# Streamed weights: low part written over the loaded words, five loaded and four rounded places, each unit split one unit earlier

## The reference

```python
# first block, each of 2 layers (z, the context, is carried too in the first)
x = x + 0.5 * mx[2] * swiglu(modulate(rms_norm(x), mx[0], mx[1]), ffn1_w1[l], ffn1_w3[l], ffn1_w2[l])
hx = modulate(rms_norm(x), mx[3], mx[4]) @ w_in[l]
...                                   # neighbourhood, gated linear, grouped-query attention, Fourier mixing
x = x + mx[5] * (mix_x @ w_out[l])
x = x + 0.5 * mx[8] * swiglu(modulate(rms_norm(x), mx[6], mx[7]), ffn2_w1[l], ffn2_w3[l], ffn2_w2[l])
# second block, each of 2 layers
h = h + jnp.einsum('blc,cd->bld', mix, w_out)          # forgetting attention and retention
h = h + swiglu of rmsnorm(h)
```

## Time and profile before

| what | value |
|---|---|
| median of 3 runs | 2449.03 (2448.18 to 2449.29) |
| span of the profiled execution | 2444.0 |
| PE busy | 2386.3 (98%) |
| DVE busy | 1510.9 (62%) |
| ACT busy | 1002.4 (41%) |
| POOL busy | 394.3 (16%) |
| share of PE in the chain that ended last | 90% |
| mean granted TensorE clock | 0.998 |

### The profile page before, as it was taken

The page is one execution under the profiler, slowest core; times in us unless marked ns, Lnnn a source line. Parts: engine busy times, 40 slices in busy tenths (PEclk is TensorE's granted clock), DMA queues, the critical chain, the costliest instruction groups (busy, mean ns, idle before and its releaser), DMA issues.

```text
span 2444.0 us, 39330 instructions
## 1 busy us (share of the span) xinstructions
PE 2386.3 (98%) x15054; PEld 2096.5 (86%) x15054; DVE 1510.9 (62%) x2546; ACT 1002.4 (41%) x1645; POOL 394.3 (16%) x403
## 2 busy tenths in 40 slices
PE   7999999999999999999999999999999999999998
PEld 4888888777888888888888878999888999989998
DVE  5878765784699855523323585665666665666664
ACT  4222334644522223422222465545445444446443
POOL 2221211240122221111011130121000220000220
PEclk9999999999999999999999999999999999999999
DMA  8566542112366664233322222555433555434554
GB/s 330 196 210 212 177 150 87 61 61 82 105 222 230 241 219 155 87 96 102 96 95 95 87 78 77 185 181 183 151 110 128 173 173 179 148 114 139 190 189 138
DMA packets 97879, 362.49 MB, mean 148 GB/s; under 512 B 11024, under 2 KB 11280, under 8 KB 96560
## 3 DMA queue, kind: packets, MB, share of 16 engines
q1 hardware_dynamic: 75744, 274.42, 34.0%
q0 software_dynamic: 21968, 85.72, 10.2%
HBM read 359.04 MB, written 1.05 MB: 147 GB/s over the span
## 4 chain that ended last, share of the span: by engine, by line
PE 90%; DVE 3%; ACT 3%; issue 2%; DMA 1%; POOL 0%; ACTq 0%; DVEq 0%; POOLq 0%
PE bank L746 28%; PE bank L748 27%; PE bank L747 27%; ACT ring_high L1241 1%; PE bank L1026 1%; DVE ring_low L1713 1%; PE bank L996 1%; PE bank L1014 1%; PE bank L1048 1%; PE bank L967 0%; PE bank L975 0%; DMA arena<-w_mod_first_dram 0%; PE bank L1191 0%; PE bank L1104 0%; DVE arena L1779 0%
## 5 line engine op out<-in xcount | busy, mean ns | idle before, releaser
L1713 DVE TENSOR_TENSOR ring_low<-ring,ring_high 128x1024 fp32r<-128x1024 f32 x524 | 649.9, 1240 | 553.1 <-ACT ring_high L1241 551.1
L746 PE MATMUL bank<-x_parts,ring_high 128*128 128x512 f32 (+2 forms) x2700 | 912.4, 338 | 14.2 <-DVE ring_low L1713 10.5
L748 PE MATMUL bank<-x_parts,ring_low 128*128 128x512 f32 (+2 forms) x2700 | 899.8, 333 | 0.0
L747 PE MATMUL bank<-x_parts,ring_high 128*128 128x512 f32 (+2 forms) x2700 | 898.6, 333 | 0.0
L1241 ACT ACTIVATE ring_high<-ring 128x1024 fp32r<-128x1024 f32 x524 | 551.6, 1054 | 628.9 <-PE bank L748 628.4
L746 PEld LDWEIGHTS bank<-x_parts,ring_high 128*128 128x128 f32 x2700 | 510.1, 189 | 80.3 <-issue 18.1
L748 PEld LDWEIGHTS bank<-x_parts,ring_low 128*128 128x128 f32 x2700 | 510.2, 189 | 48.1
L747 PEld LDWEIGHTS bank<-x_parts,ring_high 128*128 128x128 f32 x2700 | 510.1, 189 | 47.0 <-issue 0.2
L609 POOL TENSOR_TENSOR hidden_parts<-fresh,hidden_parts 128x512 fp32r<-128x512 f32 (+2 forms) x132 | 215.0, 1628 | 1354.5 <-ACT hidden_parts L1360 1354.5
L746 PE MATMUL bank<-hidden_parts,ring_high 128*128 128x512 f32 (+2 forms) x1122 | 368.1, 328 | 0.3 <-POOL hidden_parts L609 0.3
L748 PE MATMUL bank<-hidden_parts,ring_low 128*128 128x512 f32 (+2 forms) x1122 | 367.3, 327 | 0.0
(11 more groups left out here) (232 smaller groups left out, 2130.0 us busy)
## 6 DMA issues: line engine op xcount, KB each, us to landing
ring<-stream_dram SPq DMA_DIRECT2D x521, 512.0 KB, 3.4
mod_ring<-w_mod_dram POOLq DMA_DIRECT2D x128, 512.0 KB, 4.8
arena<-w_mod_first_dram POOLq DMA_DIRECT2D x8, 1024.0 KB, 10.3
ring<-stream_dram POOLq DMA_DIRECT2D x3, 512.0 KB, 10.7
arena<-na_bias_dram POOLq DMA_DIRECT2D x2, 768.0 KB, 11.4
mod_ring<-consts_dram POOLq DMA_DIRECT2D x1, 1140.0 KB, 5.4
resid<-x_dram POOLq DMA_DIRECT2D x2, 512.0 KB, 6.0
resid<-ctx_dram POOLq DMA_DIRECT2D x2, 512.0 KB, 7.2
```

The source lines that it names most:

```text
L746: pe.matmul(out, w[0][:, b], xh, start=start, stop=False)
L747: pe.matmul(out, w[0][:, b], xl, start=False, stop=False)
L748: return pe.matmul(out, w[1][:, b], xh, start=False, stop=stop)
L1713: dve.tensor_tensor(low[:, u % RING], ring[:, u % RING], high_f[:, u % RING], ALU.subtract).then_inc(low_parts, 1)
```

## The change

It keeps five places for loaded words and four for the rounded high part. The low part is written over the loaded words, so the ring takes nine places in SBUF as before. ACT and DVE split up to four units ahead. SP loads unit u when PE has used unit u - 5. SP's loop over the stream becomes straight-line code. At the start, two units instead of one are split before the first ffn1 goes on.

```diff
-RING = 3
+LOADED = 5
+SPLIT = 4
+FIRST_UNITS = 3
...
-        ring = sb("ring", RING * UNIT).rearrange("p (s n) -> p s n", s=RING)
-        high = sb("ring_high", RING * UNIT, F32R)
-        low = sb("ring_low", RING * UNIT, F32R)
+        ring = sb("ring", LOADED * UNIT).rearrange("p (s n) -> p s n", s=LOADED)
+        low = sb("ring_low", LOADED * UNIT, F32R, over=place_of["ring"]).rearrange("p (s n) -> p s n", s=LOADED)
+        high = sb("ring_high", SPLIT * UNIT, F32R)
...
-            turns = UNITS // RING
-            with sp.Fori(1, turns) as turn:
-                for s in range(RING):
-                    sp.wait_ge(low_parts, turn * RING + (s + 1 - RING))
-                    sp.dma_start(ring[:, s], A["stream"][turn * RING + s]).then_inc(unit_loaded[s], 16)
...
+            for u in range(FIRST_UNITS, UNITS):
+                if u >= LOADED:
+                    sp.wait_ge(*when("unit_used", u - LOADED))
+                sp.dma_start(ring[:, u % LOADED], A["stream"][u]).then_inc(unit_loaded[u % LOADED], 16)
...
-                while split[0] < min(split[1] + RING, UNITS):
+                while split[0] < min(split[1] + SPLIT, UNITS):
                     u = split[0]
                     split[0] += 1
-                    if u >= RING:
-                        act.wait_ge(*when("unit_used", u - RING))
+                    if u >= SPLIT:
+                        act.wait_ge(*when("unit_used", u - SPLIT))
...
-                    dve.tensor_tensor(low[:, u % RING], ring[:, u % RING], high_f[:, u % RING],
+                    dve.tensor_tensor(low[:, u % LOADED], ring[:, u % LOADED], high_f[:, u % SPLIT],
                                       ALU.subtract).then_inc(low_parts, 1)
...
-                    split_ahead(1)
+                    split_ahead(2)
```

More of the change, by code:

```diff
@@ L262, in build @@
         eps_one = sb("eps_one", 2)
-        ring = sb("ring", RING * UNIT).rearrange("p (s n) -> p s n", s=RING)
-        high = sb("ring_high", RING * UNIT, F32R)
-        low = sb("ring_low", RING * UNIT, F32R)
-        high_f = high.bitcast(F32).rearrange("p (s n) -> p s n", s=RING)
-        high = high.rearrange("p (s n) -> p s n", s=RING)
-        low = low.rearrange("p (s n) -> p s n", s=RING)
+        ring = sb("ring", LOADED * UNIT).rearrange("p (s n) -> p s n", s=LOADED)
+        low = sb("ring_low", LOADED * UNIT, F32R, over=place_of["ring"]).rearrange("p (s n) -> p s n", s=LOADED)
+        high = sb("ring_high", SPLIT * UNIT, F32R)
+        high_f = high.bitcast(F32).rearrange("p (s n) -> p s n", s=SPLIT)
+        high = high.rearrange("p (s n) -> p s n", s=SPLIT)
         xr = sb("x_parts", 2 * KC * N1, F32R)
@@ L353, in scalar2 @@
             return small[0:rows, at:at + 1]
-        unit_loaded = [sem(f"unit_loaded{i}") for i in range(RING)]
+        unit_loaded = [sem(f"unit_loaded{i}") for i in range(LOADED)]
         high_parts = sem("high_parts")
@@ L560, in _ @@
             sp.wait_ge(*when(f"first_mod_loaded{(KC - 1) % FIRST_SLOTS}", KC - 1))
-            turns = UNITS // RING
-            with sp.Fori(1, turns) as turn:
-                for s in range(RING):
-                    sp.wait_ge(low_parts, turn * RING + (s + 1 - RING))
-                    sp.dma_start(ring[:, s], A["stream"][turn * RING + s]).then_inc(unit_loaded[s], 16)
-            for u in range(turns * RING, UNITS):
-                sp.wait_ge(low_parts, u - RING + 1)
-                sp.dma_start(ring[:, u % RING], A["stream"][u]).then_inc(unit_loaded[u % RING], 16)
+            for u in range(FIRST_UNITS, UNITS):
+                if u >= LOADED:
+                    sp.wait_ge(*when("unit_used", u - LOADED))
+                sp.dma_start(ring[:, u % LOADED], A["stream"][u]).then_inc(unit_loaded[u % LOADED], 16)
             for g in range(2):
@@ L741, in weights @@
                 pe.wait_ge(low_parts, u + 1)
-                return [w[:, u % RING].rearrange("p (b n) -> p b n", b=8) for w in (high, low)]
+                return [w[:, u % n].rearrange("p (b n) -> p b n", b=8) for w, n in ((high, SPLIT), (low, LOADED))]
             def product(out, w, b, xh, xl, start, stop):
@@ L874, in late_products @@
                                 mean_square(tag, 0)
-                assert len(held) <= RING
+                assert len(held) <= SPLIT
             def ffn(tag, n, parts, prev):
@@ L1231, in split_ahead @@
                 split[1] += used
-                while split[0] < min(split[1] + RING, UNITS):
+                while split[0] < min(split[1] + SPLIT, UNITS):
                     u = split[0]
                     split[0] += 1
-                    if u >= RING:
-                        act.wait_ge(*when("unit_used", u - RING))
-                    if u < RING:
+                    if u >= SPLIT:
+                        act.wait_ge(*when("unit_used", u - SPLIT))
+                    if u < FIRST_UNITS:
                         act.wait_ge(*when(f"first_unit_loaded{u}", u))
                     else:
-                        act.wait_ge(unit_loaded[u % RING], 16 * (u // RING))
-                    act.activation(high[:, u % RING], ring[:, u % RING], ACT.Copy).then_inc(high_parts, 1)
+                        act.wait_ge(unit_loaded[u % LOADED], 16 * (u // LOADED + (u % LOADED >= FIRST_UNITS)))
+                    act.activation(high[:, u % SPLIT], ring[:, u % LOADED], ACT.Copy).then_inc(high_parts, 1)
             def ln_exp():
@@ L1658, in _ @@
             first_rows(0)
-            split_ahead(1 - RING)
+            split_ahead(1 - SPLIT)
             act.wait_ge(*when("mean", ("start",)))
@@ L2350, in _ @@
                     split_ahead(1)
+            split_ahead(1)
             for l in range(DEPTH):
```

## The result

The changed kernel takes 2454.14 us (median of 8 runs, 2450.9 to 2460.14), the kernel before 2448.61 us (8 runs, 2446.34 to 2450.68). The ratio is 1.003, 95% interval 1.0021 to 1.0039: slower, by about 0.3%. The profiled execution has a span of 2451.9 us, before 2444.0.

A forecast was written before the change was run, and what follows sets the result against it. PE bounds the kernel, busy 2386.3 of 2444.0 us, so only its waits can give, at most 12.1 us. Costs of 8.0 less gains of 3.3 make +4.7 on 2449.03: 2453.7 us, +0.19%, range 2449.5 to 2457.5.

The forecast's parts named there:

- First and second unit of the four stages: Starts of the four stages keeping x and context apart: the 1.17 us wait becomes a wait for the norm, gain 0.
- third unit: Same four stages: the 0.96 us wait goes, but POOL's chunks let only 0.3 of 1.1 us be kept, four times.
- Rival 2: More is kept at the third units because POOL's real ends are earlier: up to 3.2 us more, 2450.5 us; chance 0.14.
- Fourth unit of the first ffn2: PE gains 1.64 us at 658.36 but waits that much longer for the hidden part at 769.02: gain 0.
- Fourth unit in the other two: First ffn1 (0.44 us) and second layer's ffn2 (1.53 us): waits go, with refill a gain of 2.1 us.
- First mixing: ACT's second rounding waits for its load, so the squares and PE's second mean come late: cost 2.06 us.
- Second layer's mixing: The second rounding is 2.27 us late there, delaying the squares and PE's next unit: cost 1.9 us.
- b2 twice: Late rounding and low part delay DVE's queue to L1952, which PE waits for: cost 2.0 us each, 4.0 together.
- Out projections, ffns, narrow stages: Roundings are late there too, but eviction banks or the distance between load and use cover it: cost 0.
- rival 3: The load lands before ACT comes to round it: no cost, gain 3.3 us, 2445.7 us; chance 0.06.
- rival 4: All 12.1 us of low-part waits go and no new wait comes: 2436.9 us; chance 0.05.
- rival 5: Late narrow-stage roundings reach norm chains (3.6 us), or close loads land after 4.5 us (4.4 us): 2457.3 to 2458.1; chance 0.23.

The follow-up runs named there:

- number 4: Changed kernel with three rounded places and rounding three units ahead instead of four, loads as in the change: 2450.86 us, ratio 1.0012 to the kernel before.
- number 5: As number 4, but each load goes out one release later, at the release of the unit four back: 2464.28 us, ratio 1.007.
- number 6: Kernel before the change, with only the rounding behind the second projection put behind the third, in first and second mixings: 2446.26 us, ratio 0.9993.
- number 1: Changed kernel with the rounding behind the second projection put behind the third, in both first mixings and both `b2`: 2440.35 us, ratio 0.997.
- number 2: Changed kernel with the rounding behind the second projection put behind the third in the two first mixings alone: ratio 1.0005.
- number 3: Changed kernel with the rounding behind the second projection put behind the third in the two `b2` alone: ratio 0.9992.
- number 7: The gates-first kernel: number 1 with, in `b2`, one of two roundings behind the third projection put behind the fourth: 2442.02 us, ratio 0.9975.
- both second times: Number 1 and number 7, each unchanged, run again on the same chip: 2441.86 us, ratio 0.9974, and 2436.79 us, ratio 0.9958.

## Why the prediction was right

It said 2453.7 us, and 2454.14 was measured. Part of that closeness is luck. Counted from the kernel before, it said 4.7 us more, and the medians differ by 5.5. Its likeliest outcome was a change of less than 0.2% (0.49), and the ratio of 1.003 lies beyond that, among the slower outcomes, to which it gave 0.46. The mechanism was right in both directions: the waits that would go, and the late second rounding that would cost. Step by step:

- *The list of PE's waits as the cap.* Right: all 12.1 us for the low part went.
- *First and second unit of the four stages, 0; third unit 0.3 each.* Right in kind: 1.17 became a wait of 0.99 at 400.42 and 0.13 more than before at 402.01 (0.62 against 0.49), and of the 1.1 at the third unit 0.7 were given back at 411.08 and 414.42, where PE waits for POOL's `x_low`. 1.5 is kept in place of 1.2. Rival 2 is out.
- *Fourth unit of the first ffn2, 0.* The step that failed, the one term put at nothing that was not nothing. In this pair of traces half of the 1.7 is kept: the wait at the hidden part grew by 0.9 us, not by 1.6. The prediction took VectorE's chain to keep its hour because between the two places it waits for nothing but the modulation's loads. That reading is right, but those waits are not fixed. The chain runs from VectorE's last wait for a release by PE, a low part, to PE's matmul on the hidden part:

```profile
656.99 1.22 DVE L1713 TENSOR_TENSOR ring_low<-ring,ring_high 128x1024 fp32r<-128x1024 f32 x1 [5.61 <-ACT ring_high L1241]
```

```profile
659.33 1.23 DVE L1710 TENSOR_TENSOR ring_low<-ring,ring_high 128x1024 fp32r<-128x1024 f32 x1 [5.34 <-ACT ring_high L1238]
```

| traces | from that low part to the hidden part | of it waits for the modulation's rows | PE's wait for the hidden part |
|---|---|---|---|
| four with three rounded places (before, numbers 4, 5, 6) | 112.0 to 112.9 | 9.0 to 10.2 | 0.23 to 1.09 |
| seven with four (after, numbers 1, 2, 3, 7 and both second times) | 110.3 to 111.1 | 7.5 to 8.4 | 0.36 to 1.18 |

With four rounded places the chain is shorter in every trace, by 1.6 us on average, and it waits about that much less for the modulation's rows. PE's wait at the hidden part alone can't tell: it is 1.18 and 0.36 in the two traces of one kernel (number 1). Counted from the stage's start to the hidden part, the four-place traces are 1.9 us shorter on average, of 2.1 that the third and fourth unit give, so the 0.85 of this pair is low for what is kept. Why those rows are waited for less is open: no run moves them by themselves.
- *Fourth unit in the other two, 2.1.* Measured 0.67 + 1.68 = 2.35.
- *Gains in sum 3.3*: measured 4.7 in this pair of traces.
- *First mixing 2.06.* Mis-sized: 2.68. The landing took 4.0 us from the release, not 3.5. "The decisive load of each pair is the first, issued alone" was wrong: the second goes out 0.4 us behind it. At this place the two landed after 3.9 and 4.8 us; the first of the other three pairs took 3.3 to 3.6.
- *Second layer's mixing 1.9*: 2.04. *b2 twice 2.0*: 2.20 and 1.86.
- *Costs in sum 8.0*: measured 8.8. Numbers 1 and 5 show both that these four are the cost and what they hang on.
- *Out projections, ffns, narrow stages 0.* Right: no new wait of PE in any of them.
- *Writing over the source costs nothing.* A low part takes 1231 ns on average against 1240.
- *Left out: the clock.* The time was said to change only where PE waits, with the clock at its upper level all through. But 2.8 us of the profiled difference are the lower level, with 1.0 more in the first 30 us. So net of gains and costs the kernel lost 4.1 us where 4.7 was said, and the close hit of the total owes something to the clock. It goes with the scatter of the runs: the kernel after covers 9 us, the one before 4, and its three slowest executions (2457.98 to 2460.14 us) have mean granted clocks of 0.991 to 0.994, the other five 0.996 or 0.997.

Rivals 3 and 4 (the load lands in time) are out by the DMA that ends ACT's wait; rival 5's narrow stages are out, its slower landings came true in part, at the first mixing (0.6 us).

## What to carry to other kernels

A ring that loads and rounds at the same counter is only as deep as the distance between the two releases; where two units are released at once that distance is zero, and a fresh load is then waited for by whatever engine rounds it. Look at what stands behind that instruction in its queue: here the cure wasn't another place but to put the work that the bound engine needs ahead of the rounding that nobody needs for three units. When a deeper buffer loses, check both sides apart before giving it up: the gain (4.7 us) was real and larger than forecast, and a change of where two roundings stand, which gives the old kernel nothing (number 6), turned 1.003 into 0.997.

## What the hardware showed that I had not expected

The granted clock falls to its lower level in stretches of 3 to 7 us whose place changes from one execution to the next. The stretch near 1427 us follows the longer wait at the squares in the kernel after, but number 4 has it without the longer wait, number 3 has the wait and not the stretch, and number 3 has one at 1008 us that no other execution has. Behind the second `b2` it came in all three executions with a wait of 3.4 to 3.8 us ahead of it (the kernel after, numbers 2 and 5), and with the wait of 1.5 us in the kernel before, number 3 and the second time of number 1, but not in number 4 and the first time of number 1, nor in number 6, where the wait is 1.0 us. So a longer wait may make it likelier (three of three against three of five with 1.5 us), which so few executions can't show; that it is needed is refuted. The two profiled executions of the gates-first kernel, 2436.2 and 2433.5 us, differ by such a stretch: 1763 to 1770 us in the one, and in the other no stretch below full clock between 27 and 2429 us. For a change of 0.2 to 0.4% this is the size of the effect, and the matching of matmuls between two traces found the gates-first kernel's gain twice, where the times of its two sets left it open.
